# A mixture-of-experts kernel on one Trainium2 core: expert outputs kept as two DRAM rows per token, or added into one DRAM row by the scattering DMA

## The chip, the core and the metric

The kernel runs on one core of one Trainium2 chip. The metric is device time in microseconds (us), the median of several executions. The core has five engines that run side by side and meet only at semaphores: TensorE (PE: matmuls, and PEld for its weight loads), VectorE (DVE), ScalarE (ACT), GpSimd (POOL) and SyncE (SP, which here issues DMAs). Sixteen DMA engines carry out what the queues of SP (q1), ACT (q10) and GpSimd (q0) hand them.

## What is computed

Two layers are applied to 384 tokens of width 1024 (128 context tokens and 256 latent tokens, in three tiles of 128). The first half of a layer (projection, three mixers, merge) is called the dense part here and the change touches it only in passing. The second half is a mixture of experts: a router picks two of 16 experts for each token, each expert is a gated network of width 512, and the token receives the sum of its two experts' outputs, each times a gate.

```python
for e in range(N_EXPERTS):                      # 16
    a = jax.nn.silu(h @ w_g[e]) * (h @ w_u[e])  # 1024 -> 512
    y = y + gates[:, e:e + 1] * (a @ w_d[e])    # 512 -> 1024, zero gate if not picked
...
x = x + gate2 * y
```

All in float32. A product is done as three matmuls of parts (high x high, high x low, low x high), so each 128x1024 chunk of weights (`raw`, 512 KB) becomes a high part (`wxh`, ACT, L1826) and a low part (`wxl`, DVE, L2466) before PE uses it (L606).

## The kernel before

Every engine has a program of its own, written out by hand in the order in which it runs; semaphores tie them together, and nothing reorders them.

**Weight stream.** SP loads the weights of an expert as 12 chunks (L550 for gate and up, L561 for down) into a ring of 6 buffers `raw`. A load is issued when DVE has made the low part of the chunk that lay there. ACT makes the high part when the chunk has landed and when PE is done with the chunk six earlier in `wxh`. So a chunk goes round DMA, ACT, DVE, SP, with PE behind it.

**Rows.** A token's place among the tokens of an expert is its slot. The router (DVE, L2414 to L2457) makes the scores, a mask of the two picks, the gates and the slots. ACT writes the normed tokens `h2` (L1781) and the gates (L1810) to DRAM rows `h2_rows`. GpSimd gathers for expert e the rows of its tokens into `xg` (`fetch_rows`, L1974), PE turns them (L615, out of `xg`), and after the expert ACT writes `oe_rows`, the output times the gate, 128 rows of 1024 of which only the used slots count (L1853). For the first 14 experts (`LOOSE`) GpSimd scatters these to DRAM (`scatter_rows`, L1984); rows of unused slots have an index beyond the bound and are dropped. `oe_rows` has two buffers, so ACT waits for the scatter of expert e-2 (semaphores `scattered0`, `scattered1`). The last two experts aren't scattered: PE adds their outputs by matmuls with one-hot matrices (L1316).

**Two rows per token.** `part_rows` in DRAM has 768 rows: row 2t is for the pick of token t with the lower expert number and 2t+1 for the other. Which of the two an expert is for its tokens is worked out in the router (L2441 to L2444: a rank in `gate[:, :, 16:32]`, carried along in `h2_rows`), and in `slot_dest` (L2493) or the second column of `slot_table`. SP fills all of `part_rows` with zeros during the dense part (L533, six DMAs a layer).

**End of a layer.** GpSimd waits for all 14 scatters, reads `part_rows` back with six DMAs of 512 KB (L2014, per tile into `y` and `y_second`) and adds the pairs (L2017, three adds). DVE waits for `parts_added` and runs `add_parts(t)`: `y` times a gate (L2596), and onto `x` (L2597). Its order there is: output of expert 14 (L2518), one-hot (L2485), `add_parts(0)`, a branch on whether an expert has more than 128 tokens (it hasn't, L405 and L406), `last_lo(0)` (L2662), `add_parts(1)`, `last_lo(1)`, then six units of y times gate and add (L2673, L2676), with `add_parts(2)` after the second. PE's L1316 for the first three units needs `last_lo(0)`, for the other three `last_lo(1)`. `last_lo` itself needs ACT's `oe_odd` (L1909), half by half.

Of the kernel before, what the change touches and what calls it, by code (L numbers as in the profile page):

```python
# [24 lines left out]
P = 128  # L25
# [127 lines left out]
def bank_of(u):  # L153
# [19 lines left out]
ROW = D + 2 * NE  # L173
# [25 lines left out]
    pick_ready=PICKED, idx_acc=PICKED, idx_ready=PICKED, table=16 * (2 * NT + 2), pickT_ready=2, scattered0=16 * LOOSE // 2, scattered1=16 * LOOSE // 2, zeroed=16 * 6, parts_in2=16 * 2, parts_added=NT, X_acc=NE + 1, xe_hi=NE + 1, xe_ready=NE + 1,  # L199
    gathered0=16 * NE // 2 + 32, gathered1=16 * NE // 2 + 32, silu_done=NE,  # L200
# [19 lines left out]
def build(nc, io):  # L220
# [21 lines left out]
    def room(size):  # L242
# [72 lines left out]
    y_second = [place("y_second0", [P, D], F32, gbc_at), place("y_second1", [P, D], F32, gbc_at + 4096),  # L315
                place("y_second2", [P, D], F32, r_z + 8192)]
# [13 lines left out]
    slot_token = place("slot_token", [P, 4, 2], F32)  # L330
    slot_dest = place("slot_dest", [P, 4], I32)
    slot_table = place("slot_table", [P, NE, 2], I32)
    no_token = place("no_token", [P, NE * 2], I32)
    table_row = place("table_row", [P, NT, 2], I32)
    table_data = place("table_data", [P, NT, 2, 2], I32)
# [31 lines left out]
    gate = place("gate", [P, NT, 2 * NE], F32)  # L367
# [8 lines left out]
    part_rows = nc.dram_tensor("part_rows", (2 * T, D), F32).ap()  # L376
    table_rows = nc.dram_tensor("table_rows", (P * NE, 2), I32).ap()
# [86 lines left out]
    def sync_program(sp):  # L464
# [49 lines left out]
        for l in range(DEPTH):  # L514
            p = DENSE0[l]
            for kind, which, half, pairs in USES:
                for k in range(pairs):
# [14 lines left out]
                    if 0 <= i < 6 and odd == 0:  # L532
                        sp.dma_start(part_rows[i * P:(i + 1) * P, :], io["t_zeros"].broadcast_to([P, D])).then_inc(sem("zeroed"), 16)  # L533
# [1410 lines left out]
    def gpsimd_program(pool):  # L1944
# [7 lines left out]
        pool.memset(ae[:, 0:2 * NE], float(NO_TOKEN)).then_inc(sem("rw_zero"), 1)  # L1952
        pool.wait_ge(sem("rw_zero"), 1)
        pool.tensor_copy(no_token[:, :], ae[:, 0:2 * NE]).then_inc(sem("rw_zero"), 1)
# [4 lines left out]
        for l in range(DEPTH):  # L1959
# [6 lines left out]
            def fetch_rows(e, k):  # L1966

                if e < PICKED:
                    pool.wait_ge(sem("idx_ready"), at("idx_ready", l, 1) + e)
                    index = slot_index[:, e:e + 1]  # L1970
                else:
                    pool.wait_ge(sem("xe_ready"), at("xe_ready", l, e))
                    index = slot_table[:, e, 0:1]
# [16 lines left out]
            pool.wait_ge(sem("zeroed"), at("zeroed", l, 16 * 6))  # L1990
# [4 lines left out]
            for t in range(NT):  # L1995
                for s in range(2):
                    pool.indirect_dma_start(table_rows[:, :],
                                            bass.IndirectOffsetOnAxis(ap=table_row[:, t, s:s + 1], axis=0),
                                            table_data[:, t, s, :], None,
# [3 lines left out]
            pool.dma_start(slot_table[:, :, :].rearrange("p e c -> p (e c)"), table_slots).then_inc(sem("table"), 16)  # L2003
# [7 lines left out]
            for t in range(NT):  # L2011
                both = part_rows[2 * P * t:2 * P * (t + 1), :].rearrange("(p s) n -> p s n", s=2)
                for s, dst in enumerate((y[:, t, :], y_second[t][:, :])):
                    pool.dma_start(dst, both[:, s, :]).then_inc(sem(PARTS_IN[t]), 16)  # L2014
            for t in range(NT):
                pool.wait_ge(sem(PARTS_IN[t]), at(PARTS_IN[t], l, PER[PARTS_IN[t]]))
                pool.tensor_tensor(y[:, t, :], y[:, t, :], y_second[t][:, :], ALU.add).then_inc(sem("parts_added"), 1)  # L2017


    def vector_program(dve):  # L2020
# [40 lines left out]
        for l in range(DEPTH):  # L2061
# [378 lines left out]
            g4 = gt.rearrange("p (g i j) -> p g i j", i=EG, j=EG)  # L2440
# [338 lines left out]
```

## Time and profile before

| | |
|---|---|
| median of 3 runs | 1649.46 us (1648.64 to 1653.35) |
| span of the profiled execution | 1646.0 us; the page gives no time around it, the median is 3.5 us above |
| PE busy | 1567.6 us |
| DVE busy | 1047.2 us |
| ACT busy | 923.8 us |
| POOL busy | 530.5 us |
| DMA traffic | 381.77 MB |
| mean granted TensorE clock | 0.984 |

The chain of waits followed back from the end is 70% PE, 12% DVE, 10% DMA, 5% ACT. The expert parts lie from about 525 to 843 us and from about 1335 to 1643 us of the span. Between them DMA is busy three to six tenths, in them nine tenths and more.

### The profile page before, as it was taken

The page shows a single profiled execution, that of the slowest core. Times are in us where ns is not written, and L with a number is a line of the kernel's source. Part 1 is how long each engine was busy: PE and PEld are TensorE (multiplying, and loading weights), DVE is VectorE, ACT ScalarE, POOL GpSimd, SP SyncE. Part 2 cuts the span into 40 slices and gives each one's busy share as a digit, 9 for nine tenths or more (in the row PEclk, how much of TensorE's full clock was granted, in tenths as well). Part 3 has the DMA queues.
Part 4 walks back from the last instruction along what each step waited for, and adds up shares of the span by engine and source line. Part 5 has one row for each costly group of instructions (what it writes and reads, how often), then busy time and mean ns, then how long its engine had stood idle before and what let it go on. Part 6 is the DMA issues. An engine that isn't in the chain of part 4 may idle for free.

```text
span 1646.0 us, 21287 instructions
## 1 busy us (share of the span) xinstructions
PE 1567.6 (95%) x7693; PEld 1234.8 (75%) x7693; DVE 1047.2 (64%) x1385; ACT 923.8 (56%) x1284; POOL 530.5 (32%) x271
## 2 busy tenths in 40 slices
PE   7999999989999999999889999999999989999996
PEld 4677778877775887888676777787767778888885
DVE  2226546673355898998862357377433479899998
ACT  3343445434335788888644343444353458888893
POOL 2344554444532111111234445444445131111112
PEclk9999999999998999999999999999999999999998
DMA  9765343344359999999946543422443469999995
GB/s 363 265 199 167 115 128 91 102 130 143 115 174 334 344 385 362 370 377 364 368 170 210 187 154 112 133 90 89 144 147 111 157 224 379 378 368 378 381 368 205
DMA packets 153822, 381.77 MB, mean 232 GB/s; under 512 B 21060, under 2 KB 26886, under 8 KB 153724
## 3 DMA queue, kind: packets, MB, share of 16 engines
q1 hardware_dynamic: 122704, 325.32, 56.2%
q10 hardware_dynamic: 20140, 36.56, 6.3%
q0 software_dynamic: 10880, 18.59, 3.1%
q8 instruction: 60, 0.98, 0.2%
q14 instruction: 38, 0.31, 0.1%
HBM read 378.55 MB, written 27.93 MB: 247 GB/s over the span
## 4 chain that ended last, share of the span: by engine, by line
PE 70%; DVE 12%; DMA 10%; ACT 5%; issue 2%; ACTq 0%; SPq 0%; POOL 0%; DVEq 0%; POOLq 0%
PE ps L606 56%; PE ps L615 4%; DVE wxl L2466 4%; DMA raw<-w_e_down 4%; DMA raw<-w_e_up 3%; PE ps L639 2%; PE ps L952 2%; ACT wxh L1826 1%; DMA own<-w_mod 1%; PE ps L980 1%; PE ps L886 1%; DVE uv L2241 1%; ACT wh L1331 1%; PE ps L658 1%; PE ps L650 1%
## 5 line engine op out<-in xcount | busy, mean ns | idle before, releaser
L1949 POOL TENSOR_TENSOR wl<-raw,wh 128x1024 fp32r<-128x1024 f32 x168 | 409.8, 2443 | 531.7 <-ACT wh L1331 531.5
L2466 DVE TENSOR_TENSOR wxl<-raw,wxh 128x1024 fp32r<-128x1024 f32 x384 | 454.5, 1220 | 55.2 <-ACT wxh L1826 52.5
L1826 ACT ACTIVATE wxh<-raw 128x1024 fp32r<-128x1024 f32 x384 | 402.6, 1061 | 92.4 <-DMA raw<-w_e_down 35.4
L606 PE MATMUL ps<-wxh,xeT 128*128 128x512 f32 x1024 | 341.3, 399 | 4.0 <-issue 2.5
L1331 ACT ACTIVATE wh<-raw 128x1024 fp32r<-128x1024 f32 x168 | 176.7, 1056 | 227.6 <-PE ps L606 223.2
L606 PE MATMUL ps<-wh,hTh 128*128 128x512 f32 x720 | 293.2, 407 | 5.9 <-DVE hTl L2088 3.3
L606 PE MATMUL ps<-wh,hTl 128*128 128x512 f32 x720 | 281.9, 392 | 0.0
L606 PE MATMUL ps<-wl,hTh 128*128 128x512 f32 x720 | 281.5, 391 | 0.0
L606 PEld LDWEIGHTS ps<-wxh,xeT 128*128 128x128 f32 x1024 | 193.3, 189 | 46.8 <-issue 4.3
L606 PE MATMUL ps<-wxl,xeT 128*128 128x512 f32 x512 | 199.9, 390 | 0.0
L606 PEld LDWEIGHTS ps<-wh,hTh 128*128 128x128 f32 x720 | 135.7, 188 | 40.7 <-issue 7.9
L606 PEld LDWEIGHTS ps<-wh,hTl 128*128 128x128 f32 x720 | 135.6, 188 | 29.6
L606 PEld LDWEIGHTS ps<-wl,hTh 128*128 128x128 f32 x720 | 135.8, 189 | 27.5 <-issue 0.5
L606 PE MATMUL ps<-wxh,eaT 128*128 128x512 f32 x480 | 153.2, 390 | 0.0
L606 PEld LDWEIGHTS ps<-wxl,xeT 128*128 128x128 f32 x512 | 96.9, 189 | 18.5 <-issue 0.5
L606 PEld LDWEIGHTS ps<-wxh,eaT 128*128 128x128 f32 x480 | 90.1, 188 | 18.7
L606 PE MATMUL ps<-wxl,eaT 128*128 128x512 f32 x240 | 93.4, 389 | 0.0
L1984 POOL DMA_INDIRECT part_rows<-oe_row_odd,slot_table x12 | 13.0, 1085 | 188.6 <-ACT oe_row_odd L1853 188.6
L606 PE MATMUL ps<-wh,mT 128*128 128x512 f32 x192 | 61.4, 397 | 0.0
L606 PE MATMUL ps<-wh,ybT 128*128 128x512 f32 x192 | 61.1, 393 | 0.0
L1671 ACT ACTIVATE aT<-ps 128x512 f32<-128x512 f32 (+1 forms) x32 | 17.4, 545 | 75.3 <-PE ps L615 75.3
L1984 POOL DMA_INDIRECT part_rows<-oe_row_even,slot_table x10 | 10.9, 1094 | 144.7 <-ACT oe_row_even L1853 144.7
(282 smaller groups left out, 2177.3 us busy)
## 6 DMA issues: line engine op xcount, KB each, us to landing
raw<-w_e_gate SPq DMA_DIRECT2D x128, 512.0 KB, 6.5
raw<-w_e_up SPq DMA_DIRECT2D x128, 512.0 KB, 5.8
raw<-w_e_down SPq DMA_DIRECT2D x128, 512.0 KB, 5.5
raw<-w_in SPq DMA_DIRECT2D x120, 512.0 KB, 3.7
own<-w_mod ACTq DMA_DIRECT2D x27, 1024.0 KB, 7.6
raw<-w_mod SPq DMA_DIRECT2D x36, 512.0 KB, 5.1
raw<-w_br_b SPq DMA_DIRECT2D x16, 512.0 KB, 3.8
raw<-w_out SPq DMA_DIRECT2D x16, 512.0 KB, 3.8
```

The source lines that it names most:

```text
L606: ins = pe.matmul(out, act_hl[i], w_hl[j], start=start and n == 0, stop=stop and n == 2)
L615: return pe.transpose(out, in_, ident[0:n, 0:n])
L639: last = pe.matmul(ps[32 * j:32 * j + 32, bank, :], cs[:, 4 * half + j, :], w[:, j, :], start=half == 0, stop=half == 1 and not (n in GATE ...
L650: last = pe.matmul(ps[:, bank, at0 + 2 * k:at0 + 2 * k + 2], modrow[:, slot, k * P:(k + 1) * P], sel2[:, :], start=True, stop=True)
L658: pe.matmul(ps[:, bank, :], selb[:, g, :], modrow[:, slot, :], start=True, stop=True).then_inc(sem("gate_acc"), 1)
L952: last = pe.matmul(out, qT[rows, t * P:(t + 1) * P], keys, start=True, stop=True)
L1331: act.activation(wh[:, p % RING, :, :], raw[:, c % RAW, :, :], ACT.Copy).then_inc(sem("hi_done"), 1)
L1671: act.activation(aT[:, 4 * i:4 * i + n, :], ps[:, 3, 0:n * P].rearrange("p (k n) -> p k n", k=n), ACT.Copy).then_inc(sem("aT_copied"), 1)
L1826: act.activation(wxh[:, q % RING_MOE, :, :], raw[:, place, :, :], ACT.Copy).then_inc(sem("hi_done"), 1)
L1949: pool.tensor_tensor(wl[:, p % RING, :, :], raw[:, PAIR_CHUNK[p] % RAW, :, :], wh[:, p % RING, :, :].bitcast(F32), ALU.subtract).then_inc( ...
L1984: pool.indirect_dma_start(part_rows[:, :], bass.IndirectOffsetOnAxis(ap=index, axis=0), oe_rows[k % 2][:, :], None, bounds_check=last_part ...
L2466: dve.tensor_tensor(wxl[:, q % RING_MOE, :, :], raw[:, expert_chunk(l, 0, q)[0], :, :], wxh[:, q % RING_MOE, :, :].bitcast(F32), ALU.subtr ...
```

## The change

`part_rows` has one row per token, 384 in all, and the scatter adds to it: the DMA reads the row in DRAM, adds the row from SBUF and writes it. Since two experts can hold the same token, the scatter of expert e now waits until that of expert e-1 has landed. The index for the scatter is that of the gather, so the rank of a pick, `slot_dest` and the second columns of the tables go. The read-back is one DMA a tile, the adds on GpSimd go, and DVE waits for the DMA itself. The zero fill is three DMAs a layer.

```diff
-ROW = D + 2 * NE
+ROW = D + NE
...
-                    if 0 <= i < 6 and odd == 0:
+                    if 0 <= i < NT and odd == 0:
                         sp.dma_start(part_rows[i * P:(i + 1) * P, :], io["t_zeros"].broadcast_to([P, D])).then_inc(sem("zeroed"), 16)
...
-                index = slot_dest[:, e:e + 1] if e < PICKED else slot_table[:, e, 1:2]
+                index = slot_index[:, e:e + 1] if e < PICKED else slot_table[:, e:e + 1]
                 pool.wait_ge(sem("out_hi"), at("out_hi", l, 1) + e)
+                if e:
+                    pool.wait_ge(sem(f"scattered{1 - k % 2}"), at(f"scattered{1 - k % 2}", l, 16 * ((e + 1) // 2)))
                 pool.indirect_dma_start(part_rows[:, :],
                                         bass.IndirectOffsetOnAxis(ap=index, axis=0),
                                         oe_rows[k % 2][:, :], None,
-                                        bounds_check=last_part, oob_is_err=False).then_inc(sem(name), 16)
-
-            last_part = pool.to_reg(2 * T - 1)
+                                        bounds_check=last_part, oob_is_err=False, compute_op=ALU.add).then_inc(sem(name), 16)
+
+            last_part = pool.to_reg(T - 1)
...
             for t in range(NT):
-                both = part_rows[2 * P * t:2 * P * (t + 1), :].rearrange("(p s) n -> p s n", s=2)
-                for s, dst in enumerate((y[:, t, :], y_second[t][:, :])):
-                    pool.dma_start(dst, both[:, s, :]).then_inc(sem(PARTS_IN[t]), 16)
-            for t in range(NT):
-                pool.wait_ge(sem(PARTS_IN[t]), at(PARTS_IN[t], l, PER[PARTS_IN[t]]))
-                pool.tensor_tensor(y[:, t, :], y[:, t, :], y_second[t][:, :], ALU.add).then_inc(sem("parts_added"), 1)
+                pool.dma_start(y[:, t, :], part_rows[t * P:(t + 1) * P, :]).then_inc(sem(PARTS_IN[t]), 16)
...
-            g4 = gt.rearrange("p (g i j) -> p g i j", i=EG, j=EG)
-            link(dve.tensor_tensor(g4, m48.rearrange("p (g j) -> p g j", j=EG).unsqueeze(2).to_broadcast([P, 12, EG, EG]),
-                                   rank_tri[:, :, :].unsqueeze(1).to_broadcast([P, 12, EG, EG]), ALU.mult))
-            link(dve.tensor_reduce(sb.rearrange("p (g i) -> p g i", i=EG), g4, AX.X, ALU.add))
-            link(dve.tensor_copy(gate[:, :, NE:2 * NE], sb.rearrange("p (t e) -> p t e", t=NT)))
...
-                dve.tensor_scalar(slot_dest[:, k % 4:k % 4 + 1], xg[:, k % 2, bass.ds(e + (D + NE), 1)], 0.5,
-                                  slot_token[:, k % 4, 1:2], ALU.is_gt, ALU.add)
...
-                dve.wait_ge(sem("parts_added"), at("parts_added", l, t + 1))
+                dve.wait_ge(sem(PARTS_IN[t]), at(PARTS_IN[t], l, PER[PARTS_IN[t]]))
```

GpSimd's program at the end of layer 0, before: `xg` is the gather, `part_rows<-oe_row` the scatter, `wl` the first work of layer 1.

```order
43 L1984 DMA part_rows<-oe_row_even,slot_table 768x1024
44 L1984 DMA part_rows<-oe_row_odd,slot_table 768x1024
45 L2014 DMA y<-part_rows 128x1024
46 L2014 DMA y_second_114<-part_rows 128x1024
47 L2014 DMA y<-part_rows 128x1024
48 L2014 DMA y_second_115<-part_rows 128x1024
49 L2014 DMA y<-part_rows 128x1024
50 L2014 DMA y_second_116<-part_rows 128x1024
51 L2017 TENSOR_TENSOR y<-y,y_second_114 128x1024
52 L2017 TENSOR_TENSOR y<-y,y_second_115 128x1024
53 L2017 TENSOR_TENSOR y<-y,y_second_116 128x1024
54 L1949 TENSOR_TENSOR wl<-raw,wh 128x1024 x84
```

The same place of the changed kernel (its lines lie up to 17 lower):

```order
42 L1972 DMA xg<-h_rows,slot_table 128x1040
43 L1984 DMA part_rows<-oe_row_even,slot_table 384x1024
44 L1984 DMA part_rows<-oe_row_odd,slot_table 384x1024
45 L2012 DMA y<-part_rows 128x1024 x3
46 L1947 TENSOR_TENSOR wl<-raw,wh 128x1024 x84
```

Three of six read-backs and all three adds are gone, and nothing of GpSimd's is left between the last scatter and layer 1 but three DMA issues.

VectorE's program in the router, from the mask to the slots, before (`rt` is scratch):

```order
303 L2437 TENSOR_TENSOR mask<-rt 128x48
304 L2441 TENSOR_TENSOR rt<-mask,rank_tri 128x192
305 L2443 TENSOR_REDUCE rt<-rt 128x48
306 L2444 COPY gate<-rt 128x3x16
307 L2445 TENSOR_TENSOR rt<-s_r,mask 128x48
308 L2446 TENSOR_REDUCE rt<-rt 128x3
309 L2447 RECIPROCAL rt<-rt 128x3
310 L2448 TENSOR_TENSOR gate<-rt 128x3x16
311 L2453 SCALAR_TENSOR_TENSOR slot<-ps,mask 128x48
```

And of the changed kernel:

```order
303 L2432 TENSOR_TENSOR mask<-rt 128x48
304 L2435 TENSOR_TENSOR rt<-s_r,mask 128x48
305 L2436 TENSOR_REDUCE rt<-rt 128x3
306 L2437 RECIPROCAL rt<-rt 128x3
307 L2438 TENSOR_TENSOR gate<-rt 128x48
308 L2443 SCALAR_TENSOR_TENSOR slot<-ps,mask 128x48
```

Three of the seven operations from the mask to the gate are gone; the slots follow the gate as before.

## Rows read from the trace of the kernel before

**Rows 1.** Page, busy time of the engines over the span

```profile
PE 1567.6 (95%) x7693; PEld 1234.8 (75%) x7693; DVE 1047.2 (64%) x1385; ACT 923.8 (56%) x1284; POOL 530.5 (32%) x271
```

**Rows 2.** Busy us by engine, one window; at the end PEclk, DMA share, GB/s

```profile
1496.40:1514.20 17.80, 17.80 (x86) 14.79 (x85) 17.03 (x18) 15.81 (x18) 2.52 (x2) 1.00 1.01 379
```

**Rows 3.** Timeline, PE turns gathered rows: first, last of each layer; start, duration

```profile
549.51 1.11 PE L615 MATMUL ps<-ident,xg 128*128 128x128 f32 x8
...
783.66 1.15 PE L615 MATMUL ps<-ident,xg 128*128 128x128 f32 x8
...
1357.96 1.11 PE L615 MATMUL ps<-ident,xg 128*128 128x128 f32 x8
...
1590.77 1.11 PE L615 MATMUL ps<-ident,xg 128*128 128x128 f32 x8
```

**Rows 4.** Waits of ACT, 540 to 790: total us, times, longest

```profile
ACT wxh L1826 <- DMA raw<-w_e_down: 15.2, 22, 2.6
...
ACT wxh L1826 <- PE ps L606: 2.9, 6, 1.3
```

**Rows 5.** GpSimd's queue, packets, MB, share: span; 567.37:585.64; 1501.81:1519.60

```profile
q0 software_dynamic: 10880, 18.59, 3.1%
...
q0 software_dynamic: 288, 0.69, 9.5%
...
q0 software_dynamic: 288, 0.12, 2.4%
```

**Rows 6.** Scatter L1984: issue to landing; DMA view: gather's median landing

```profile
DMA to landing us min/median/max: 5.8/7.1/10.3
...
xg<-h_rows,slot_table POOLq DMA_INDIRECT x26, 8.2
```

**Rows 7.** Timeline, end of layer 1: GpSimd, DVE, ACT, PE

```profile
1603.18 1.50 POOL L1984 DMA_INDIRECT part_rows<-oe_row_odd,slot_table  x1 [15.83 <-ACT oe_row_odd L1853]
1610.81 0.58 POOL L2014 DMA_DIRECT2D y<-part_rows  x1 [6.12 <-DMA part_rows<-oe_row_odd,slot_table]
...
1617.90 8.26 POOL L2017 TENSOR_TENSOR y<-y,y_second 128x1024 f32<-128x1024 f32 x3 [3.85 <-DMA y_second<-part_rows]
...
1620.54 3.41 DVE L2596 TENSOR_TENSOR y<-y,gbc 128x1024 f32<-128x1024 f32 x1
1623.98 3.27 DVE L2597 TENSOR_TENSOR x<-x,y 128x1024 f32<-128x1024 f32 x1
1628.50 0.75 DVE L2662 SCALAR_TENSOR_TENSOR oe_odd<-ps,slot_gate,oe_odd 128x512 fp32r<-128x512 f32 x1 [1.25 <-issue]
1629.16 1.22 DVE L2596 TENSOR_TENSOR y<-y,gbc 128x1024 f32<-128x1024 f32 x1
...
1621.86 0.69 ACT L1909 ACTIVATE oe_odd<-ps,slot_gate 128x512 fp32r<-128x512 f32 x1 [3.06 <-PE ps L606]
...
1629.39 1.19 PE L1316 MATMUL ps<-oe_even,pickT 128*128 128x512 f32 x2 [4.92 <-DVE oe_odd L2662]
```

**Rows 8.** Tile y, 1598 to 1630: issue to landing of its loads

```profile
DMA to landing us min/median/max: 5.8/7.2/8.7
```

**Rows 9.** Timeline, end of layer 0: DVE and PE

```profile
819.41 3.41 DVE L2597 TENSOR_TENSOR x<-x,y 128x1024 f32<-128x1024 f32 x1
...
829.23 0.80 PE L1316 MATMUL ps<-oe_even,pickT 128*128 128x512 f32 x2 [4.15 <-DVE oe_odd L2662]
```

**Rows 10.** Source L406, the branch: durations ns min/median/max, first and last start

```profile
L406 PEldq COMPARE_BRANCH  x2: 3542/4859/6176, 820.1 to 1620.9; - x2
```

**Rows 11.** Timeline, router of layer 0 and layer 1: DVE, ACT's queue

```profile
505.40 0.36 DVE L2441 TENSOR_TENSOR rt<-mask,rank_tri 128x192 f32<-128x192 f32 x1
...
506.42 0.21 DVE L2445 TENSOR_TENSOR rt<-s_r,mask 128x48 f32<-128x48 f32 x1
...
507.56 0.68 ACTq L1810 DMA_DIRECT2D h_rows<-gate  x1
...
1325.12 0.21 DVE L2453 SCALAR_TENSOR_TENSOR slot<-ps,mask 128x48 f32<-128x48 f32 x1 [3.35 <-PE ps L1108]
```

More of the change, by code:

```diff
@@ L314, in build @@
     oe_rows = [place("oe_row_even", [P, D], F32, r_ya), place("oe_row_odd", [P, D], F32, r_z)]
-    y_second = [place("y_second0", [P, D], F32, gbc_at), place("y_second1", [P, D], F32, gbc_at + 4096),
-                place("y_second2", [P, D], F32, r_z + 8192)]
+    y_over = place("y_over", [P, D], F32, gbc_at)
     oes = [place("oe_even", [P, 2, D], F32R, r_ya), place("oe_odd", [P, 2, D], F32R, r_z)]
@@ L329, in build @@
     tokens_r = place("tokens_r", [P, NT, 2], F32R)
[L330 to L333, printed above, removed]
+    slot_token = place("slot_token", [P, 4], F32)
+    slot_table = place("slot_table", [P, NE], I32)
+    no_token = place("no_token", [P, NE], I32)
     table_row = place("table_row", [P, NT, 2], I32)
-    table_data = place("table_data", [P, NT, 2, 2], I32)
+    table_data = place("table_data", [P, NT], I32)
     slot_index = place("slot_index", [P, 4], I32)
@@ L366, in build @@
     mask = place("mask", [P, NT + 1, NE], F32)
-    gate = place("gate", [P, NT, 2 * NE], F32)
+    gate = place("gate", [P, NT, NE], F32)
     cnt = place("cnt", [P, 8], F32)
@@ L2490, in own_gate @@
                 dve.tensor_copy(slot_gate[:, k % 4:k % 4 + 1], xg[:, k % 2, bass.ds(e + D, 1)])
-                if not (isinstance(e, int) and e < PICKED):
-                    return
-                dve.tensor_scalar(slot_dest[:, k % 4:k % 4 + 1], xg[:, k % 2, bass.ds(e + (D + NE), 1)], 0.5,
-                                  slot_token[:, k % 4, 1:2], ALU.is_gt, ALU.add)
             def rows_lo(e, k, count):
@@ L2558, in vector_program @@
             if l == 0:
-                for s in range(2):
-                    dve.tensor_scalar(table_data[:, :, s, 0], tokens_r[:, :, 0].bitcast(F32), float(NO_TOKEN), None, ALU.add)
-                    dve.tensor_scalar(table_data[:, :, s, 1], tokens_r[:, :, 1].bitcast(F32), float(NO_TOKEN + s), None, ALU.add)
-            place3, first3, second3 = [rt[:, i, 0:48].rearrange("p (t e) -> p t e", t=NT) for i in range(3)]
+                dve.tensor_scalar(table_data[:, :], tokens_r[:, :, 0].bitcast(F32), float(NO_TOKEN), None, ALU.add)
+            place3, first3 = [rt[:, i, 0:48].rearrange("p (t e) -> p t e", t=NT) for i in range(2)]
             link(dve.scalar_tensor_tensor(place3, slot[:, :, :], float(NE), iota[:, 0:NE].unsqueeze(1).to_broadcast([P, NT, NE]),
@@ L2565, in vector_program @@
             link(dve.tensor_tensor(first3, place3, mask[:, 0:NT, :], ALU.mult))
-            link(dve.tensor_tensor(second3, first3, gate[:, :, NE:2 * NE], ALU.mult))
             link(dve.tensor_reduce(rt[:, 3, 0:3], first3, AX.X, ALU.add))
-            link(dve.tensor_reduce(rt[:, 3, 3:6], second3, AX.X, ALU.add))
+            link(dve.tensor_reduce(rt[:, 3, 3:6], first3, AX.X, ALU.max))
             dve.tensor_tensor(table_row[:, :, 0], rt[:, 3, 0:3], rt[:, 3, 3:6], ALU.subtract)
@@ L2646, in turn @@
                     wait_pe(OVER_PE["part"] + c)
-                    dve.scalar_tensor_tensor(y_second[0][:, cols], ps[:, 4 + c % 2, :], cnt[:, 5 + t:6 + t], gbc[:, 1, min(t, 1), cols],
+                    dve.scalar_tensor_tensor(y_over[:, cols], ps[:, 4 + c % 2, :], cnt[:, 5 + t:6 + t], gbc[:, 1, min(t, 1), cols],
                                              ALU.mult, ALU.mult).then_inc(over_dve, 1)
                     dve.wait_ge(over_dve, over_at("dve", e, b, OVER_DVE["part"] + 2 * c))
-                    dve.tensor_tensor(x[:, t, cols], x[:, t, cols], y_second[0][:, cols], ALU.add).then_inc(over_dve, 1)
+                    dve.tensor_tensor(x[:, t, cols], x[:, t, cols], y_over[:, cols], ALU.add).then_inc(over_dve, 1)
                 dve.wait_ge(over_dve, over_at("dve", e, b, OVER_STEPS["dve"]))
```

30 lines of the change are left out of this document (15 added, 15 removed).

## The prediction, made before the changed kernel was run

> **What bounds the kernel now.** I read the page first: PE is busy 1567.6 of 1646.0 us [rows 1]. Where the change acts, the question is what PE waits for, so I cut the expert parts into windows of one expert. PE is busy in all 17.80 us of such a window and the DMA engines' share is 1.01 at 379 GB/s [rows 2]: PE and the weight stream run level. How level, PE's turning of gathered rows shows, which comes once an expert. From the first to the last of layer 0 go 234.15 us for 13 experts, of layer 1 232.81 [rows 3]; PE's own work is 17.80 each, 231.4. PE loses 2.75 and 1.4 us to the stream and has no more to give. The waits say the same: ACT waited 15.2 us in 22 times for landing down weights alone, and for PE only 2.9 us in 6 [rows 4]. The buffers are never all full, and whatever takes DMA time in the expert parts comes nearly whole to PE.
>
> How much GpSimd's rows take: its queue moved 18.59 MB, of which the 12 read-backs of 0.52 MB are 6.29, and 60 gathers and scatters share the rest, 0.205 MB each. The expert at 567.37 with 0.69 MB of such rows held 9.5% of the DMA engines for 18.27 us, 1.74 us; that at 1501.81 with 0.12 MB held 2.4% of 17.79 us, 0.43 us [rows 5]. The difference is 2.3 us per MB. The first of these windows is 0.5 us longer than PE's work, the second not longer.
>
> Last I read the end of a layer, where the added rows return. In layer 1 GpSimd issues the last scatter at 1603.18, the read-backs from 1610.81, and adds from 1617.90 for 8.26 us. DVE's two operations of add_parts(0) fall into these adds and take 3.41 and 3.27 us, where the same form takes 1.22 beside an idle GpSimd. After them come the branch and last_lo(0) at 1628.50; PE, idle 4.92 us, starts 0.14 us after its end [rows 7].
>
> **The end of layer 1.** Without the adds add_parts(0) takes 2.5 us from 1620.54 in place of 6.7, so last_lo(0) starts 4.2 us sooner, near 1624.3. ACT's half is ready by 1622.55, and PE's branch, 3.54 us from 1620.9, ends at 1624.5 [rows 7, 10], so neither is in the way. All that follows is DVE's own sequence: **-4.1 us**. Beside the trace's row the Trainium skill (SBUF — State Buffer, on the shared port pair) says that a VectorE instruction with two SBUF inputs and a GpSimd instruction that reads SBUF exclude each other for the whole of an instruction; that is what the two long rows show.
>
> What is late next: the tile must have landed by 1620.54. The read-back was issued 7.6 us after the scatter; one load then lands in 5.8 us [rows 7, 8], at 1616.6. That leaves 3.9 us for a slower scatter before this gain shrinks.
>
> **The end of layer 0.** The second operation of add_parts(0) took 3.41 us beside GpSimd, 2.2 too many. But PE started L1316 only at 829.23 [rows 9], since its branch, begun at 820.1, took 6.18 us [rows 10] and a later fetch followed while the DMA engines were full of read-backs and the next layer's weights. With 1.57 MB less in the queue (4.1 us at 379 GB/s) the fetch and the last down weights may come sooner. Between nothing and 4.1 I take **-2 us**.
>
> **The router.** Three DVE operations go, 505.40 to 506.42, 1.0 us. But ACT issues the gates only at 507.56, after its own last row copy, and in layer 1 the slots wait 3.35 us for PE [rows 11]. So this is hidden; its cover gone, it would be 1.0 us a layer. The operation slot_dest before the first rows of an expert is on the path at a tenth of a microsecond: **-0.3 us** for both layers with the shorter slot operations. Six zero fills of 512 KB fewer lie in the dense parts, where the DMA engines are busy three to six tenths: 0. The gather's rows are 4160 bytes in place of 4224 and the tables half as wide: 0, since their packets stay as many.
>
> **The added wait.** On GpSimd the scatter of e now waits for that of e-1, and behind it stands the gather of e+4. Scatters come 17.8 us apart and land in 5.8 to 10.3 [rows 6]. Even if an adding scatter takes its own 7.1 and a gather's 8.2 us one after the other, 15.3, it has landed: **0**.
>
> **The adding scatter.** No row shows one. From below it costs nothing more: it writes the same bytes, and the read of DRAM goes in the shadow of that. The nearest row for the read is the gather, which reads DRAM rows of the same size: the scatter then costs itself and one gather. That is 28 scatters x 0.205 MB x 2.3 us = 13.2 us of DMA time. From above, if a DMA engine also stands still between read and write of each row, three times a scatter: 26 us. I take the middle one, as the row that does what is added. Of it layer 0, where PE lost in most experts, pays all, 6.6 us; layer 1, where the stream gained in the last seven, pays half, 3.3. With no lead gained either way: **+10 us** (0 to 13 for the middle price, up to 26 x 0.75 = 20 for the upper).
>
> The Trainium skill (Collectives: The Full Stack, on the bandwidth ceiling) speaks against this change too: the add in a DMA is free, but it needs two source reads on one ring, which halves the rate. By it the scatter would double, the same 13.2 us; no row of this kernel shows it.
>
> **Sum** against the profiled execution: 1646.0 - 4.1 - 2 - 0.3 + 10 = 1649.6 of span, and with the 3.5 us by which the median stands above the span, **1653 us**. This is 0.2% above the median; a measurement of this kernel tells about 0.3%, 4.9 us, from no change.
>
> **The rivals.** *The read is hidden* (faster): the sum without its last term but 0 to 3 us, 1643 to 1646. For it: writes alone may set the scatter's time, and 0.205 MB in 6.7 MB an expert is 3%. Against: DMA share at 1.01, and the heavier window is the longer one. *The add is dear* (slower): more than 1.5 times the middle price, from 5 us more on, gives 1658 to 1670. For it: read, add and write of each row hang together on one engine, and chunks of weights queue behind. Against: the DMA engines have several queues to serve meanwhile. *The serial wait binds*: if an adding scatter takes over 17.8 us, ACT's oe_rows and the gathers stand behind it; each microsecond over costs one in 26 experts, 1675 and more. Against are the 15.3 us above. *The ends don't gain*: if the scatter lands 8.2 us later, the tile lands at 1624.8, 4.2 after its need, and the gain of layer 1 is gone: with a hidden read in the stream 1649, otherwise 1657.
>
> **How the numbers follow.** The middle price 0.43 (1647 to 1659; of it 0.29 within 0.3% and 0.14 slower), the hidden read 0.27 (0.22 faster, 0.05 within), the dear add 0.20 (slower), the serial wait 0.04 (slower), no gain at the ends 0.06 (0.05 within, 0.01 faster). Faster 0.23, same 0.39, slower 0.38. The range leaves about one in ten at each side: 1642 to 1666. The likeliest case alone is 1647 to 1659.
>
> **What would show it.** In the profile after: DVE's y and x operations of add_parts(0) at 1.22 us in both layers, and last_lo(0) of layer 1 about 2.5 us plus the branch after the one-hot; DVE's chain from there to the end as long as before. PE's turnings 18.2 to 18.6 us apart in place of 18.0 and 17.9. The share of GpSimd's queue in a window with 0.5 to 0.7 MB up by some 3 to 4 points, and scatters that land in 8 to 12 us. The prediction is wrong if the turnings keep their pace (the hidden read), or if GpSimd's idle time before a scatter is ended by the scatter before it (the serial wait), or if DVE waits for the read-back at add_parts(0). It is wrong by size if the turnings are 19 us apart or more.

## The result, and the profile after

The changed kernel takes **1665.35 us** (median of 5 runs, 1662.36 to 1671.0) where the kernel before takes 1649.38 beside it: ratio 1.0095, 95% interval 1.0076 to 1.0115. It is slower by 16 us. A second set of runs of it (e9, below) gave 1.0088 (1.0066 to 1.0109). The forecast was 1653, with 1642 to 1666 as its range; the result lies at that range's upper end, 0.65 us inside it, and outside the 1647 to 1659 of its likeliest case. It is the case that had 0.20 there, the dear add; that the range holds it is little more than luck.

The profiled execution has a span of 1663.6 us, 17.6 more than before. The page of the changed kernel, busy times and GpSimd's queue:

```profile
PE 1570.6 (94%) x7693; PEld 1231.3 (74%) x7693; DVE 1042.4 (63%) x1362; ACT 923.1 (55%) x1284; POOL 515.8 (31%) x259
...
q0 software_dynamic: 10016, 15.32, 3.4%
```

GpSimd's queue moved 3.3 MB less than before and yet took more of the span, 3.4% for 3.1% [rows 5]. Next come the rows of the timeline that answer to [rows 3], PE's turning of gathered rows in the changed kernel. The first row of a layer is its third turning, expert 2's; before layer 1's, its second turning stands here too:

```profile
550.02 1.11 PE L613 MATMUL ps<-ident,xg 128*128 128x128 f32 x8
...
792.81 1.11 PE L613 MATMUL ps<-ident,xg 128*128 128x128 f32 x8
...
1352.51 1.11 PE L613 MATMUL ps<-ident,xg 128*128 128x128 f32 x8
...
1369.74 1.11 PE L613 MATMUL ps<-ident,xg 128*128 128x128 f32 x8
...
1610.62 1.11 PE L613 MATMUL ps<-ident,xg 128*128 128x128 f32 x8
```

From the first to the last of layer 0 there are now 242.79 us in place of 234.15, in layer 1 240.88 in place of 232.81. These 13 experts a layer cost **+8.6 and +8.1 us**, nearly all of the 17.6. The other parts: all up to the second turning of layer 0 -0.5; from there to the third 14.97 us, +1.0; from layer 0's last turning to layer 1's first -1.8; from there to layer 1's third +4.4, of which its second distance has 17.23 us in place of 12.83; from layer 1's last turning to the end of the program 52.98 in place of 55.23, -2.25.

What stood in PE's way shows in the waits of ACT between 540 and 800 us, the same experts as 540 to 790 before (total, times, longest):

```profile
ACT wxh L1824 <- DMA raw<-w_e_gate: 33.7, 47, 2.3
ACT wxh L1824 <- DMA raw<-w_e_down: 8.9, 13, 2.2
```

Before, ACT waited 15.2 us for down weights [rows 4], and in the same view 14.8 for gate weights; now it waits 33.7 for gate weights and 8.9 for down weights. The DMA view of three windows, each from one turning to the next (GpSimd's queue: packets, MB, share of 16 engines), is from 567.80 to 586.92, from 681.52 to 700.89 and, with few rows, from 1518.44 to 1536.34:

```profile
q0 software_dynamic: 288, 0.69, 14.1%
...
q0 software_dynamic: 288, 0.48, 9.9%
...
q0 software_dynamic: 288, 0.12, 3.3%
```

The first answers to [rows 5]: the same 0.69 MB, 9.5% then, 14.1% now. A layer's 13 windows begin with its third turning, and scatters fall into the last 12. Added up over these the queue's busy time went from 12.72 to 19.51 us and from 12.92 to 19.91, +13.8 us in all. PE lost 16.7. A scatter now lands after 8.2 us, a gather after 8.8 [rows 6 has 7.1 and 8.2]. The tile view of `part_rows` and the DMA view:

```profile
DMA to landing us min/median/max: 4.6/8.2/11.5
...
xg<-h_rows,slot_table POOLq DMA_INDIRECT x26, 8.8
```

The end of layer 1 in the timeline, the counterpart of [rows 7]:

```profile
1624.97 1.58 POOL L1984 DMA_INDIRECT part_rows<-oe_row_odd,slot_table  x1 [16.37 <-ACT oe_row_odd L1851]
1632.57 1.72 POOL L2012 DMA_DIRECT2D y<-part_rows  x3 [6.02 <-DMA part_rows<-oe_row_odd,slot_table]
...
1642.36 1.22 DVE L2579 TENSOR_TENSOR y<-y,gbc 128x1024 f32<-128x1024 f32 x1
1643.61 1.23 DVE L2580 TENSOR_TENSOR x<-x,y 128x1024 f32<-128x1024 f32 x1
1646.08 0.75 DVE L2645 SCALAR_TENSOR_TENSOR oe_odd<-ps,slot_gate,oe_odd 128x512 fp32r<-128x512 f32 x1 [1.25 <-issue]
...
1646.98 0.70 PE L1314 MATMUL ps<-oe_even,pickT 128*128 128x512 f32 x2 [0.44 <-DVE oe_odd L2645]
```

DVE's two operations take 1.22 and 1.23 us, and from the first of them to last_lo(0) it is 3.72 us where it was 7.96: the 4.2 us are there. GpSimd's idle time ahead of the scatter is ended by ACT's `oe_row`, not by the scatter before it. The end of layer 0, the counterpart of [rows 9], and PE's branch, that of [rows 10]:

```profile
827.46 1.22 DVE L2579 TENSOR_TENSOR y<-y,gbc 128x1024 f32<-128x1024 f32 x1
828.71 1.22 DVE L2580 TENSOR_TENSOR x<-x,y 128x1024 f32<-128x1024 f32 x1
...
836.04 1.01 PE L1314 MATMUL ps<-oe_even,pickT 128*128 128x512 f32 x2 [6.05 <-DVE oe_odd L2645]
...
L404 PEldq COMPARE_BRANCH  x2: 3719/4978/6236, 826.6 to 1643.0; - x2
```

DVE's two operations are at 1.22 us here too, but PE starts L1314 9.4 us after its branch began (826.6), where it was 9.1 before (820.1 to 829.23). What DVE saves does not show at this start.

### The profile page after: what moved, and what is told of

The parts are those of the page before. It is cut to its first block, busy times and chain, and to the rows that moved or that the text cites. A ratio compares the mean times of both kernels' runs of the same rounds, so it can differ in the third digit from the quotient of the medians.

```text
span 1663.6 us, 21272 instructions
## 1 busy us (share of the span) xinstructions
PE 1570.6 (94%) x7693; PEld 1231.3 (74%) x7693; DVE 1042.4 (63%) x1362; ACT 923.1 (55%) x1284; POOL 515.8 (31%) x259
## 4 chain that ended last, share of the span: by engine, by line
PE 57%; DMA 16%; DVE 15%; ACT 5%; issue 5%; ACTq 0%; POOL 0%; SPq 0%; DVEq 0%
PE ps L604 44%; DMA raw<-w_e_up 8%; DVE wxl L2456 7%; DMA raw<-w_e_down 4%; PE ps L613 3%; PE ps L637 3%; ACT wxh L1824 2%; PE ps L950 2%; DMA raw<-w_e_gate 2%; PE ps L978 1%; PE ps L884 1%; ACT wh L1329 1%; DVE uv L2236 1%; PE ps L656 1%; PE ps L648 1%
## 5 line engine op out<-in xcount | busy, mean ns | idle before, releaser
L604 PEld LDWEIGHTS ps<-wxh,xeT 128*128 128x128 f32 x1024 | 193.9, 189 | 63.9 <-DVE wxl L2456 13.2
L604 PEld LDWEIGHTS ps<-wxl,xeT 128*128 128x128 f32 x512 | 97.1, 190 | 18.2 <-issue 0.5
L1984 POOL DMA_INDIRECT part_rows<-oe_row_odd,slot_table x12 | 19.0, 1586 | 200.0 <-ACT oe_row_odd L1851 200.0
L1984 POOL DMA_INDIRECT part_rows<-oe_row_even,slot_table x10 | 16.0, 1597 | 149.0 <-ACT oe_row_even L1851 149.0
```

The lines of the kernel that those rows point to most:

```text
L604: ins = pe.matmul(out, act_hl[i], w_hl[j], start=start and n == 0, stop=stop and n == 2)
L1984: pool.indirect_dma_start(part_rows[:, :], bass.IndirectOffsetOnAxis(ap=index, axis=0), oe_rows[k % 2][:, :], None, bounds_check=last_part ...
```

## The experiments

Each was timed in 5 rounds against the kernel before on the same chip. The ratio to before and its 95% interval are given. A "window" is the stretch from one of PE's turnings to the next, a "stream" the 13 of a layer as above. Each diff is cut to the lines that carry the edit.

**e1: the tables wide again.** The start of layer 1 had lost 4.4 us, and there GpSimd waits for the narrow table.

```diff
-    table_rows = nc.dram_tensor("table_rows", (P * NE, 1), I32).ap()
+    table_rows = nc.dram_tensor("table_rows", (P * NE, 2), I32).ap()
-                                            table_data[:, t:t + 1], None,
+                                            table_data[:, t, :], None,
```

> The changed kernel with its table rows in DRAM two numbers (8 bytes) wide again, as before the change; the adding scatter and its wait stay. If the 4-byte rows stall the DMA engines at the start of the experts (theory of the narrow table), the distance from the first to the second transposes of gathered rows falls from 15.0 to about 14 us in layer 0 and from 17.2 to about 13 us in layer 1, and the time falls by 4 to 5.5 us: 1660 to 1661 for 1665. If the table's row width costs nothing, as the prediction's sum had it, and the later second expert comes from something else (the scatters' order, the loads' place in the queue), the time stays at 1665 and both distances stay.

1668.35 us, 1.0097 (1.0066 to 1.0128): no gain. The timeline of GpSimd at the read-back of the table, layer 1, first of the changed kernel:

```profile
1353.83 0.60 POOL L2003 DMA_DIRECT2D slot_table<-table_rows  x1 [3.59 <-DMA table_rows<-table_data,table_row]
```

and of e1:

```profile
1357.03 0.60 POOL L2003 DMA_DIRECT2D slot_table<-table_rows  x1 [0.26 <-DMA table_rows<-table_data,table_row]
```

The narrow rows do land later. The tile view of `table_rows`, issue to landing, of the changed kernel and of e1:

```profile
DMA to landing us min/median/max: 3.8/6.7/10.7
...
DMA to landing us min/median/max: 2.1/3.8/6.8
```

Over all kernels whose view gives it the median is 5.4 to 7.0 us with 4 bytes and 3.8 to 5.1 with 8. In layer 1 GpSimd waited for these rows 2.2 to 3.8 us in the eight kernels with rows of 4 bytes, 0 to 1.3 in the six with rows of 8. In layer 0 the wait is 0 to 3.6 us with 4 bytes, 0 to 1.4 with 8, and the first profile of the changed kernel has none. But in e1 the stretches from the second turning to the third, shorter by 5.4 us together, were followed by streams longer by 3.8, and the time is the same. The theory of the narrow table fell as the cause of the loss.

**e2: no add.** A later row overwrites an earlier one, so this kernel leaves out the sum of a token's two expert rows; it is there for its time alone.

```diff
-                                        bounds_check=last_part, oob_is_err=False, compute_op=ALU.add).then_inc(sem(name), 16)
+                                        bounds_check=last_part, oob_is_err=False).then_inc(sem(name), 16)
```

> The changed kernel with a plain scatter in place of the adding one, the wait for the scatter before it kept; the output leaves out the sum of a token's two expert rows (the later row overwrites). If the add is what holds the DMA engines (theory of the dear add), the 12 full expert distances of each layer fall back by 7 to 8 us a layer, the scattering queue's busy time in them from 19.5 to about 13 us, and the time to 1649 to 1651. If the serial wait is what costs, only the scatters' busy time falls and the distances stay at 18.6 us in the mean, the time above 1662.

1643.93 us, **0.9962 (0.9945 to 0.9979)**. The layers' streams take 233.41 and 233.05 us, the queue's busy time is 12.66 and 12.81. So without its add the change would be a gain of 6 us, and the add alone costs 1.33% of 1649.4 us, 22 (1.0095 less 0.9962). The wait, which is still there, costs nothing.

**e3: the serial wait alone, in the kernel before.**

```diff
                 pool.wait_ge(sem("out_hi"), at("out_hi", l, 1) + e)
+                if e:
+                    pool.wait_ge(sem(f"scattered{1 - k % 2}"), at(f"scattered{1 - k % 2}", l, 16 * ((e + 1) // 2)))
```

> The kernel before, its two rows per token and plain scatter as they are, with only the changed kernel's wait of each scatter for the scatter ahead of it. If the wait costs nothing because scatters are 18 us apart and land in 6 to 12 us, the time stays within 0.1% of before (1648 to 1651). If the wait delays the gathers behind it on GpSimd and so the experts (rival of the serial wait), it rises by 5 us or more, above 1654.

1650.33 us, 0.9995 (0.9977 to 1.0014), streams of 234.14 and 232.91 us. The serial wait fell as a rival: with plain scatters by this time, and with adding ones by the changed kernel's idle time above, which `oe_row` ends.

**e4: the same rows on other partitions.** A slot's partition is a matter of one constant table, which the one-hot compare reads. Here slot s stands on the partition whose seven bits are those of s in reverse.

```diff
-                    ins = dve.tensor_scalar(pick[:, k % 2, t, :], iota[:, 0:P], slot[:, t, bass.ds(e, 1)], None, ALU.is_equal)
+                    ins = dve.tensor_scalar(pick[:, k % 2, t, :], iota[:, T:T + P], slot[:, t, bass.ds(e, 1)], None, ALU.is_equal)
...
-            pool.dma_start(slot_table[:, :], table_slots).then_inc(sem("table"), 16)
+            pool.indirect_dma_start(slot_table[:, :], None, table_slots,
+                                    bass.IndirectOffsetOnAxis(ap=turn_col[:, :], axis=0),
...
+    turned = np.array([int(format(n, "07b")[::-1], 2) for n in range(P)])
```

> The changed kernel with an expert's slots laid on the partitions in bit-reversed order, so that its 48 or so live rows stand all over the 128 partitions and not on the first 48; the table is read back through an indirect DMA that undoes the order. Same bytes, same rows, same instructions but that one. If the scatter's live rows sit on few of the 16 DMA engines, and the slowest engine then delays each weight chunk (theory of uneven engines), the stream of experts gets 4 us or more shorter in each layer, and the time falls to 1650 to 1658. If the rows are dealt to the engines whatever their partition, or the stall comes with each packet and not with its place, nothing changes: 1663 to 1667, perhaps 1 us more for the indirect read-back.

1647.99 us, **0.9987 (0.9969 to 1.0005)**: the loss against the kernel before is gone. The gain of e2 is not reached; e4 stays 0.25% above e2, 4 us. This is the main reading. Take in each kernel the window in which expert 6 of layer 0 (60 rows) is scattered; the windows view (PE, PEld, DVE, ACT, GpSimd busy, then clock, DMA share, GB/s) and the DMA view, of the changed kernel:

```profile
681.52:700.89 19.37, 18.44 (x85) 14.75 (x85) 16.83 (x17) 15.27 (x17) 2.72 (x3) 1.00 1.00 361
...
q0 software_dynamic: 288, 0.48, 9.9%
```

of e2:

```profile
678.71:696.66 17.95, 17.95 (x85) 14.60 (x84) 16.08 (x17) 14.88 (x17) 2.37 (x2) 1.00 1.00 368
...
q0 software_dynamic: 288, 0.48, 7.1%
```

of e4:

```profile
680.24:698.05 17.81, 17.81 (x86) 14.87 (x84) 16.27 (x16) 14.62 (x17) 2.62 (x2) 1.00 1.01 383
...
q0 software_dynamic: 288, 0.48, 12.0%
```

The bytes are equal. In e4 the adding scatter takes the engines no less than in the changed kernel, rather more (12.0% for 9.9%), and PE loses nothing: 17.81 us for 19.37, with 383 GB/s for 361. Over the layers the queue is busy for 20.14 and 20.42 us, more than the 19.51 and 19.91 of the changed kernel, and the streams take 234.02 and 235.90. So what the add takes of the DMA engines in the mean is not what PE pays; it matters on which partitions the rows stand. ACT's waits in e4, 540 to 790:

```profile
ACT wxh L1825 <- DMA raw<-w_e_gate: 15.5, 41, 1.4
ACT wxh L1825 <- DMA raw<-w_e_down: 13.9, 17, 3.3
```

They are back near the 14.8 and 15.2 us of before. The gate weights are the loads that the change makes late. The DMA view from 540 to 800 (KB each, median us to landing), of before, the changed kernel and e4:

```profile
raw<-w_e_gate SPq DMA_DIRECT2D x56, 512.0 KB, 6.5
...
raw<-w_e_gate SPq DMA_DIRECT2D x56, 512.0 KB, 7.5
...
raw<-w_e_gate SPq DMA_DIRECT2D x56, 512.0 KB, 6.7
```

**e5 and e6: two other orders**, with every instruction of e4. In place of e4's line for `turned` stands in e5 the first of these, in e6 the second:

```diff
+    turned = P - 1 - np.arange(P)
...
+    turned = np.arange(P) % 16 * 8 + np.arange(P) // 16
```

> The kernel of the spread slots (e4) with another order in its constant table: slot s stands on partition 127 - s, so that the live rows lie together again, on the last 48 partitions. Every instruction is that of e4, the indirect read-back too. If it was the spreading of live rows that gave e4 its 17 us, they are lost again: 1662 to 1668, and expert distances of 18.6 us in the mean. If it was anything else in e4 (the indirect read-back of the table, the wider constant, a shift in the queue), the time stays at 1646 to 1651.

> As e5, with slot s on partition 16 (s mod 8) + s div 8: the live rows in eight runs of six partitions, each at the start of a block of 16, so 12 live rows in each quarter of the partitions, but six in every other block of eight. If each DMA engine serves one block of eight partitions (theory of blocks), the most loaded engine has 6 rows, against 8 on the first partitions and 3 in bit-reversed order, and the time lies between, nearer to the changed kernel: 1656 to 1662. If what counts is only that the rows lie in all four quarters or apart from each other, it is that of e4: 1646 to 1651.

e5: 1676.55 us, 1.0170 (1.0141 to 1.0199). e6: 1672.03 us, 1.0139 (1.0108 to 1.0170). Neither the indirect read-back nor being in all quarters of the partitions heals anything. Both even lose more than the changed kernel (1.0095), 0.75 and 0.44% of the time before. The two expectations of 6 rows in a block were made with the mean of 48 rows an expert. The router's choices, computed from the reference's inputs, are uneven: 90, 27, 102, 45, 76, 40, 60, 14, 64, 41, 57, 8, 59, 10 rows for the 14 scattered experts of layer 0, and in layer 1 101, 29, 93, 45, 81, 37, 54, 16, 80, 43, 59, 12, 41, 10. (The trace agrees: 102 rows scattered at 4096 bytes and 60 gathered at 4160 are 0.67 MB, which the queue shows in the window from 604.85.) With 60 rows e6 puts 8 in every other block of eight, as many as the first partitions hold.

**e7: the kernel before with e4's order.** The diff is e4's.

> The kernel before with the spread slots of e4 and nothing else. Its plain scatters lose about 5 us a layer less than the adding ones. If uneven engines cost it something too, the expert distances that stand above 17.95 us (18.27, 18.32 and 18.92 in layer 0) fall to 17.8 to 17.9, and the time by 1 to 4 us: 1645 to 1649. If plain scatters are short enough to hide on whatever engines, nothing: 1649 to 1651, with up to 1 us lost at the read-back.

1645.3 us, 0.998 (0.996 to 1.000), streams of 233.13 and 233.19: at most the few microseconds expected. Plain scatters hide nearly as well in any order.

**e8: e4 and e1 together.**

> The changed kernel with both the spread slots of e4 and the 8-byte table rows of e1. If the narrow table's wait (GpSimd waited 3.8 us for its scatters in layer 1 of e4 and 0.3 us in e1) reaches the end of the program once the stream no longer hides it, the distance from the first to the second transposes of layer 1 falls from 14.3 to about 13 us and the time to 1645 to 1647, faster than before. If other waits cover it, as they did in e1, the time is that of e4, 1647 to 1649.

1645.76 us, 0.9978 (0.9957 to 0.9998). Between e4 and e8 the measurement can't tell.

**e9: the changed kernel again.**

> The changed kernel as it is, beside the three that follow on the same chip and for the distance from the first to the second transposes of layer 1, which was 17.2 us in its first profile and 12.8 to 14.3 us in every other. If that 17.2 belongs to the kernel, it stands here again; if it was one execution's, 13 to 14.5 us. Time 1661 to 1672.

1665.7 us. The timeline of its second and third turnings of layer 1:

```profile
1358.37 1.11 PE L613 MATMUL ps<-ident,xg 128*128 128x128 f32 x8
...
1371.47 1.11 PE L613 MATMUL ps<-ident,xg 128*128 128x128 f32 x8
```

13.10 us and not 17.23: that part of the first profile's loss belonged to one execution, while the whole time is the same. Its streams are 243.60 and 241.26 us, as in the first.

**e10 and e11: even blocks.** Three slots in each block of eight partitions, then one more each; and six in each, block after block. The first line is e10's, the second e11's, the third stands in both:

```diff
+    places = np.concatenate([[8 * b + c for b in range(16) for c in cs] for cs in ((0, 1, 2), (3,), (4,), (5,), (6,), (7,))])
...
+    places = np.concatenate([[8 * b + c for b in range(16) for c in cs] for cs in (range(6), (6, 7))])
...
+    turned = np.argsort(places)
```

> e4 with another order: slots 0 to 47 in threes on the first three partitions of each block of eight, the next 16 on the fourth partition of each, and so on. Neighbouring slots stay neighbours, and their tokens' rows in DRAM ascend, but each block of eight partitions has as many live rows as in e4 (4 for an expert with 50 to 64 rows, 6 or 7 for the two largest). Theory of blocks (each DMA engine serves eight neighbouring partitions, and its count of live rows is what costs): 1646 to 1652, as e4. If e4 gained because rows that are neighbours in DRAM no longer follow each other on an engine: 1660 or more.

> e10 with six slots in a block instead of three, filled block after block: an expert with 60 live rows has ten blocks of six, where the first partitions have eight blocks of eight (all but the last full) and e10 has sixteen of four. Theory of blocks, by the most loaded engine: between the two, 1654 to 1662. If only the number of engines that share the rows counts, it is nearer the changed kernel, 1660 to 1665; if six rows on an engine are still hidden, 1646 to 1652.

e10: 1666.36 us, 1.0100 (1.0074 to 1.0126). e11: 1670.69 us, 1.0123 (1.0095 to 1.0151). The window of expert 6 in e10:

```profile
683.06:703.08 20.02, 18.44 (x86) 14.75 (x85) 16.75 (x17) 15.27 (x17) 2.72 (x3) 1.00 0.96 348
...
q0 software_dynamic: 288, 0.48, 9.8%
```

The theory of blocks of eight fell: e10 has four rows in every block, as e4, and loses what the changed kernel loses. That is also what e10's rival foresaw, that e4 gained because rows that are neighbours in DRAM no longer follow each other on an engine. e6 speaks against it: neighbouring partitions hold slots eight apart there, and the loss stands. No run was made for this rival alone.

What the six orders have in common is this. The windows of the adding kernels in which an expert with 54 to 64 rows is scattered take on average:

```
order of the slots            kernels      windows  mean us
as they come                  after,e1,e9    15     19.39
from the last partition down  e5              5     19.56
runs of eight in sixteens     e6              5     19.30
threes in blocks of eight     e10             5     19.28
sixes in blocks of eight      e11             5     19.31
bits reversed                 e4,e8          10     17.83
(plain scatters, as they come before,e2,e3   15     17.93)
```

The windows of experts with 8 to 16 rows take 17.8 to 17.9 us on average in every order. So one order of six frees the experts of about 60 rows, and small experts cost nothing anywhere. The large experts, 76 to 102 rows, are not freed: 18.7 us on average in e4 and e8 (14 windows), 19.3 with the slots as they come (21) and 18.2 with plain scatters (21).

The kept traces also say how evenly a chunk of weights lands. Each load of `raw` raises its semaphore in 16 updates (1568 for the 98 loads of one buffer), and the time from the first of the 16 to the last is a measure that does not need any rule of partitions. In the same windows of experts with 54 to 64 rows its median is:

```
                                                   loads   median us
adding, as they come (after, e1, e9)                 184      3.2
adding, four other orders (e5, e6, e10, e11)         245      3.1
adding, bits reversed (e4, e8)                       119      1.6
plain, as they come (before, e2, e3)                 180      2.8
plain, bits reversed (e7, e12)                       124      1.2
```

So the order of the partitions does decide how late the last piece of a chunk is. But plain scatters as they come land nearly as unevenly as adding ones and lose next to nothing, so the unevenness alone is not the loss: it takes the add as well.

The Trainium skill (DMA: Bandwidth & Descriptors, on the descriptor swizzle) has a rule under which the orders fall apart in this way. It says of a transfer to 128 partitions that an engine serves four neighbouring partitions and the four that lie 32 further on, the first eight engines the lower 64 partitions, the others the upper. By that rule 60 rows as they come lie on 8 of the 16 engines, 8 rows each; on 8 engines in e10 too, 8 each, since threes and fours in blocks of eight fall on every other engine; in e5, e6 and e11 the fullest engine has 8 too; and with bits reversed every engine has at most 4. An expert of 14 rows has 4 on the fullest engine as they come. Counted for all 24 windows of the nine profiles with adding scatters (the changed kernel, e1, e4, e5, e6, e8 to e11):

```
live rows on the fullest engine, by that rule:   up to 4    5 to 7      8
windows                                              68        21     127
mean us                                           17.89     18.35   19.10
```

PE's own work is 17.80. Of the 68 windows one is over 18.1 us, of the 127 windows 114 are. (Large counts mostly belong to large experts; the table of orders above holds the size of the expert fixed.) The rule was laid against the windows after the last run, so it fits what was measured and was not tested by a run made for it. It leaves three things open. Expert 2 of layer 0 has 102 rows, by the rule 8 on an engine in e4 as well, and that window took 17.83 us; expert 0 of layer 1, with 101 rows, took 17.82 in the changed kernel itself. With plain scatters as they come the counts are the same 8, and nearly nothing is lost. And the rule has no reason why e5 and e6 lose more than the changed kernel.

**e12: the adds on DVE.** The kernel before with e4's order, and the pair adds on DVE in place of GpSimd.

```diff
-                pool.tensor_tensor(y[:, t, :], y[:, t, :], y_second[t][:, :], ALU.add).then_inc(sem("parts_added"), 1)
...
-                dve.wait_ge(sem("parts_added"), at("parts_added", l, t + 1))
+                dve.wait_ge(sem(PARTS_IN[t]), at(PARTS_IN[t], l, PER[PARTS_IN[t]]))
+                link(dve.tensor_tensor(y[:, t, :], y[:, t, :], y_second[t][:, :], ALU.add))
```

> e7 (the kernel before with spread slots: two rows a token, plain scatters) with the three adds of row pairs moved from GpSimd to DVE, in add_parts. By the prediction's term for the end of layer 1, tile 0 took 6.7 us there of which 3 x 1.22 us would be left once GpSimd is not at the SBUF port: 3 us gained at the end of layer 1 and up to 2 at that of layer 0, less 1.2 us for each later tile's add where it is not hidden, in all 1 to 4 us below e7: 1641 to 1645, below both kernels. If the 3.41 us of DVE's operations beside GpSimd's adds had another cause (the load of the rows, the DMA writing into the tiles), they stay at 3.4 us and nothing is gained.

1647.83 us, 0.9979 (0.9959 to 0.9999), e7's ratio again. DVE in the timeline at the end of layer 1, of e7:

```profile
1617.94 3.43 DVE L2600 TENSOR_TENSOR y<-y,gbc 128x1024 f32<-128x1024 f32 x1
1621.41 3.25 DVE L2601 TENSOR_TENSOR x<-x,y 128x1024 f32<-128x1024 f32 x1
...
1639.61 0.69 DVE L2680 TENSOR_TENSOR x<-x,y 128x512 f32<-128x512 f32 x1
```

and of e12:

```profile
1622.41 1.22 DVE L2597 TENSOR_TENSOR y<-y,y_second 128x1024 f32<-128x1024 f32 x1
1623.67 1.23 DVE L2598 TENSOR_TENSOR y<-y,gbc 128x1024 f32<-128x1024 f32 x1
1624.93 1.23 DVE L2599 TENSOR_TENSOR x<-x,y 128x1024 f32<-128x1024 f32 x1
...
1643.64 0.69 DVE L2678 TENSOR_TENSOR x<-x,y 128x512 f32<-128x512 f32 x1
```

Three operations now take 3.7 us where two took 6.7: with no GpSimd add beside them all are at 1.22 to 1.23. The 3.0 us are won, and DVE's two later adds, 1.25 us each, stand on its own chain and give 2.5 back: from the first of these operations to the start of the last 21.23 us, in place of 21.67.

## Why the prediction missed by 12 us

The kinds of cost were right, the size of one term was not. The prediction's steps, in its order.

**What bounds the kernel** was right: PE and the weight stream run level, and whatever delays the stream comes to PE. One sentence of it was too coarse, that what takes DMA time "comes nearly whole to PE". The plain scatters' own time did not (e2's 25.5 us of the queue beside 3.7 us lost in the two streams), and that of e4's adding ones neither (40.6 us of the queue beside 7.1 us lost).

**The end of layer 1, -4.1 us**: right in its mechanism and its size, 7.96 us down to 3.72; e12 separates the cause, GpSimd's adds beside DVE's. From the last turning to the end of the program e2 won 4.0 us (51.19 for 55.23) and e4 4.6, but the changed kernel only 2.25. Its last weights came late too: ACT waited 4.4 us for down weights from the last turning on, where it was 2.5 before and 2.7 in e2 and e4. The tile was not late, as foreseen.

**The end of layer 0, -2 us**: in the first pair of profiles -1.8 from the last turning of layer 0 to the first of layer 1. Over all profiles that part takes 547.1 to 549.0 us with GpSimd's adds and 545.3 to 549.3 with adding scatters or e2's, so a gain of 2 us isn't shown.

**The router, the fills and the tables, -0.3 us**: no run shows another sum. "Tables half as wide: 0" stands in the time (e1, e8), though its reason was wrong: the packets stay as many, but with 4 bytes each they land later (a median of 6.7 us in the changed kernel, 3.8 in e1), and in layer 1 GpSimd waits for them. What became of that wait is not followed further; no time shows it.

**The added wait, 0**: right, by e3 and e2.

All of these without the add are e2: the sum without its last term was -6.4 us, and e2 measured 0.38% of 1649.4, -6.3 (-3.5 to -9.1). The interval is too wide to confirm the terms one by one, and the 2 us of layer 0's end are not shown, so part of this agreement may be luck.

**The adding scatter, +10 us: the step that failed, by size.** It was two factors. The DMA time, "itself and one gather", 13.2 us for 28 scatters, was nearly right: +13.8 measured in 24 windows, which hold 1274 of the 1394 scattered rows, and the share of a window with 0.5 to 0.7 MB went up by 2.7 to 6.3 points, where 3 to 4 were foreseen. (The Trainium skill, Collectives: The Full Stack, on the bandwidth ceiling, has the add cost a second read; the queue's time agrees with it.) The share of it that PE pays, all in layer 0 and half in layer 1, was wrong: it paid 8.6 and 8.1 us in the streams for 6.8 and 7.0 us of DMA time, and with the late ends and starts 22 us by e2. The argument took the 16 engines as one resource with a mean share. ACT starts on a chunk only when the last of its 16 updates has come, and e4 shows that the mean share does not price that: 7.4 and 7.5 us of DMA time more than before, 0 and 3 us lost. That the add is the cause is shown by e2. That the loss depends on the order of the partitions is shown by e4 against e5, with the same instructions, and that the order makes the last piece of a chunk late by the 16 updates. That a few engines stand behind eight adding rows each, and that the loss goes by the rows of the fullest engine, fits most of the 216 windows and is argued.

**The rivals.** The dear add is what came, by its price; its reason, that read, add and write of a row hang together on one engine with chunks queued behind, goes well with the order's effect but isn't shown. The hidden read fell with the queue's share, the serial wait with e3. That the ends don't gain is refuted by the 3.72 us.

"Wrong by size if the turnings are 19 us apart or more": they average 18.7 and 18.5, and in the windows of experts with 54 rows and more they are 18.5 to 21.0 but for one of 17.8.

## What to carry to other kernels

When a transfer is added beside a stream that just keeps up, do not price it by its mean share alone: find out which partitions hold rows that really move, and whether the pieces of the stream's chunks still land together. An indirect DMA whose live rows fill the first partitions can be spread by permuting a constant; here that was worth 17 us, more than the change itself could win (6). The order has to be tried, for four other permutations won nothing. Work taken off GpSimd and put on DVE's chain must be shorter than what its absence frees: 3.0 us won and 2.5 paid were no gain, where doing away with the operation won 4.2.

Of the versions that compute the reference none is clearly below the kernel before by more than 0.3%; e7, e8 and e12, at 0.998, are the lowest, and can't be told from each other.

## What was unexpected

- An adding scatter holds the engines for about 50% more of the queue's time in a window with its gather (9.5% of 18.27 us to 14.1% of 19.12 for 0.69 MB), and GpSimd is busy 1.59 us to issue it in place of 1.00. In a plain scatter the order of the rows moved little (e7), in an adding one 17 us.
- With bits reversed the adding rows take more of the engines in the mean (12.0% for 9.9%) and delay less.
- Table rows of 4 bytes in place of 8, equally many, landed later (medians of 5.4 to 7.0 us for 3.8 to 5.1) and made GpSimd wait 2.2 to 3.8 us in layer 1; none of it showed in the time.
- A chunk's 16 updates are spread over 2.8 us by plain scatters on the first partitions and over 3.2 by adding ones; only the second costs time.
- Still open: why single windows with over 100 rows lost nothing, why e5 and e6 lose more than the changed kernel, and whether an order with at most 4 rows an engine but of another shape does as well. None of this was followed up.
